# Three one-pass products of split operands for the mixer projections and the embedding gate

## What is computed

```python
h = h + 0.5 * swiglu(rmsnorm(h, ffn1_norm), w_gate, w_up, w_down)    # stage ffn1
u = rmsnorm(h, mix_norm) @ w_in                                      # stage mix1, inputs
c_q, c_kv, k_rope, m_x, m_v, m_o, m_if, f_in = split_cols(u)         # 384,256,64,256,256,256,16,256
y = concat([mla(c_q, c_kv, k_rope), mlstm(m_x, m_v, m_o, m_if), fnet(f_in)])
h = h + y @ w_out                                                    # stage mix1, outputs
h = h + 0.5 * swiglu(rmsnorm(h, ffn2_norm), ...)                     # stage ffn2
e = rmsnorm(p @ ple_w_proj, ple_post_norm)                           # stage ple
h = h + sigmoid(rmsnorm(h, ple_gate_norm) @ ple_w_gate) * e
```

## Time and profile before

| | us |
|---|---|
| median of the runs | 3188.19 |
| the profiled execution | 3193.88 |
| its span, first to last instruction | 3192.1 |
| TensorE busy | 3150.0 (99%) |
| VectorE busy | 1949.2 (61%) |
| ScalarE busy | 1276.8 (40%) |
| float32 products of `xn` and `ring`, 128x256, records | 768 |

### The profile page before, as it was taken

The page is one execution under the profiler, slowest core; times in us unless marked ns, Lnnn a source line. Parts: engine busy times, 40 slices in busy tenths (PEclk is TensorE's granted clock), DMA queues, the critical chain, the costliest instruction groups (busy, mean ns, idle before and its releaser), DMA issues.

```text
span 3192.1 us, 53025 instructions
## 1 busy us (share of the span) xinstructions
PE 3150.0 (99%) x21274; PEld 2685.9 (84%) x21274; DVE 1949.2 (61%) x2974; ACT 1276.8 (40%) x1999; POOL 97.3 (3%) x106
## 2 busy tenths in 40 slices
PE   9999999999999999999999999999999999999999
PEld 8997889889778988888788888878887888876899
DVE  6755574774457556767776677557744676346444
ACT  5444454553345462222544344442224222244433
POOL 0000000000010010000000000000000000000000
PEclk9999999999999999999999999999999999999999
DMA  7543454454345435545222000035532444221353
GB/s 270 184 146 142 175 185 171 178 186 157 139 172 179 176 119 190 185 171 191 93 80 80 3 3 3 28 127 190 205 124 79 171 186 183 97 74 40 134 183 131
DMA packets 62489, 441.25 MB, mean 138 GB/s; under 512 B 6769, under 2 KB 8945, under 8 KB 9329
## 3 DMA queue, kind: packets, MB, share of 16 engines
q1 hardware_dynamic: 60992, 437.39, 37.6%
q10 hardware_dynamic: 1328, 1.46, 0.1%
HBM read 437.77 MB, written 1.05 MB: 137 GB/s over the span
## 4 chain that ended last, share of the span: by engine, by line
PE 91%; DVE 4%; ACT 3%; issue 1%; DMA 0%; POOL 0%; DVEq 0%; ACTq 0%; SPq 0%; POOLq 0%
PE ps_high L526 47%; PE ps_low L526 43%; PE ps_high L535 1%; ACT sb_w_split L774 1%; DVE sb_w_split L811 0%; DVE sb_arena L2151 0%; PE ps_low L535 0%; DVE sb_x_split L2908 0%; ACT sb_arena L2816 0%; DVE sb_silu L2926 0%; ACT sb_xn L2807 0%; DMA sb_ring<-weights 0%; DVE sb_arena L2114 0%; DVE sb_rinv L4495 0%; ACT sb_arena L1972 0%
## 5 line engine op out<-in xcount | busy, mean ns | idle before, releaser
L774 ACT ACTIVATE sb_w_split<-sb_ring 128x2048 fp32r<-128x2048 f32 x260 | 498.6, 1918 | 890.6 <-PE ps_low L526 697.5
L811 DVE TENSOR_TENSOR sb_w_split<-sb_ring,sb_w_split 128x2048 fp32r<-128x2048 f32 x260 | 597.6, 2298 | 257.1 <-ACT sb_w_split L774 257.1
L526 PE MATMUL ps_low<-sb_x_split,sb_w_split 128*128 128x512 f32 (+1 forms) x3520 | 691.2, 354 | 8.3 <-DVE sb_w_split L811 4.0
L526 PE MATMUL ps_high<-sb_x_split,sb_w_split 128*128 128x512 f32 (+1 forms) x3520 | 686.9, 353 | 0.3 <-DVE sb_w_split L811 0.3
L526 PEld LDWEIGHTS ps_low<-sb_x_split,sb_w_split 128*128 128x128 f32 x3520 | 579.0, 189 | 108.0 <-DVE sb_x_split L2908 6.0
L526 PEld LDWEIGHTS ps_high<-sb_x_split,sb_w_split 128*128 128x128 f32 x3520 | 580.3, 189 | 94.7 <-DVE sb_w_split L811 0.6
L526 PE MATMUL ps_low<-sb_a_split,sb_w_split 128*128 128x256 f32 (+1 forms) x2112 | 370.2, 325 | 0.0
L526 PE MATMUL ps_high<-sb_a_split,sb_w_split 128*128 128x256 f32 (+1 forms) x2112 | 365.7, 323 | 0.0
L526 PEld LDWEIGHTS ps_low<-sb_a_split,sb_w_split 128*128 128x128 f32 x2112 | 314.2, 190 | 37.6 <-DVE sb_w_split L811 2.6
L526 PEld LDWEIGHTS ps_high<-sb_a_split,sb_w_split 128*128 128x128 f32 x2112 | 314.9, 190 | 30.9
L1024 DVE SCALAR_TENSOR_TENSOR sb_rest<-sb_ring,sb_consts 128x1024 f32<-128x1024 f32 x256 | 313.3, 1224 | 27.1 <-DVE sb_rest L1024 7.7
(11 more groups left out here) (404 smaller groups left out, 3221.0 us busy)
## 6 DMA issues: line engine op xcount, KB each, us to landing
sb_ring<-weights SPq DMA_DIRECT2D x412, 1024.0 KB, 4.8
sb_consts<-consts SPq DMA_DIRECT2D x1, 2148.0 KB, 18.3
sb_sq<-xT SPq DMA_DIRECT2D x1, 1024.0 KB, 5.6
sb_ring<-weights SPq DMA_DIRECT2D x2, 512.0 KB, 7.5
sb_h<-ctxT ACTq DMA_DIRECT2D x1, 1024.0 KB, 15.5
out<-sb_h SPq DMA_DIRECT2D x1, 512.0 KB, 3.0
sb_vectors<-vectors ACTq DMA_DIRECT2D x1, 269.0 KB, 5.8
out<-sb_h SPq DMA_DIRECT2D x1, 256.0 KB, 2.6
```

The costliest lines, as they stand in the source:

```text
L526: ins = self.g.nc.tensor.matmul(out, lhsT, rhs, start=start, stop=stop)
L774: g.nc.scalar.activation(g.w_split[:, 0, s % 2, :], g.ring[:, n % SLOTS, :], ACT.Copy).then_inc(g.sem["w_high"], 1)
L811: g.nc.vector.tensor_tensor(g.w_split[:, 1, s % 2, :], g.ring[:, n % SLOTS, :], g.w_split[:, 0, s % 2, :].bitcast(F32), ALU.subtract).then ...
```

## The change

In mix1 and ple of the first block, the dense chunks are multiplied with `mm3`. ScalarE splits off the high part into whatever space is free (`w_split`, `a_split`, or a region of the arena, `gates_high`); VectorE writes the low part back over the chunk in its ring slot (`ring_low` is the ring's memory as fp32r). TensorE still releases the slot. The arena's buffers are put in another order so that the new region is free. The new splits are put into the lists by hand. The chunk with the gate columns stays float32; its x is used as two float32 products, high and low.

```diff
+def mixer_split_scalar(act, l, m, first, splits):
+    n = first + MIXER_CHUNKS[m]
+    act.wait_ge(g.landed[n % SLOTS], 16 * (n // SLOTS + 1))
+    if m == 0: act.wait_ge(g.sem["split_used"], splits - 1)
+    elif m == 1: act.wait_ge(g.used[(first - 1) % SLOTS], (first - 1) // SLOTS + 1)
+    elif m == 2: act.wait_ge(g.sem["split_used"], splits)
+    else: act.wait_ge(g.sem["mixer_used"], MIXER_SPLITS * l + m - 1)
+    g.nc.scalar.activation(mixer_high(g, splits, m), g.ring[:, n % SLOTS, :], ACT.Copy)...
+def mixer_split_vector(dve, m, first, splits):
+    dve.wait_ge(g.sem["mixer_high"], dve.due("mixer_high"))
+    g.nc.vector.tensor_tensor(g.ring_low[:, n % SLOTS, :], g.ring[:, n % SLOTS, :],
+                              mixer_high(g, splits, m).bitcast(F32), ALU.subtract)...
+def mixed_high(act, k, source):     # ScalarE: high part of mixed tile k; mixed_low the same on VectorE
...
 # plain_ffn_scalar, behind setup_scalar and after_down
     if kind == "ffn1":
-        plain_prepare_scalar(act, g.vec(f"mix_norm{l}"), ready, split=False)
+        for m in (1, 0):
+            mixer_split_scalar(act, l, m, act.chunks + FFN_CHUNKS, act.splits + FFN_CHUNKS)
+        plain_prepare_scalar(act, g.vec(f"mix_norm{l}"), ready, split=True)
     else:
+        ple_split_scalar(act, 0, act.chunks + FFN_CHUNKS, act.splits + FFN_CHUNKS)
...
 # plain_ffn_vector, behind setup_vector
+    if kind == "ffn1":
+        for m in (1, 0):
+            mixer_split_vector(dve, m, dve.chunks + FFN_CHUNKS, dve.splits + FFN_CHUNKS)
+    else:
+        ple_split_vector(dve, 0, dve.chunks + FFN_CHUNKS, dve.splits + FFN_CHUNKS)
     for j in range(KT):
         residual_add(dve, j, ...)
+        if j:
+            plain_low_parts(dve, g.vec(f"{name}{l}"), j - 1, target, l)
+    plain_low_parts(dve, g.vec(f"{name}{l}"), KT - 1, target, l)
...
 # mix1_tensor: gate columns (x split in two float32 products), every dense chunk, and the outputs
-            pe.mm(tile[...], xn[:, k, t * P:(t + 1) * P], w[:, k * 16:k * 16 + GATE_SPREAD], ...)
+            for n, x in enumerate(mixer_x(g, k, slice(t * P, (t + 1) * P))):
+                pe.mm(tile[...], x.bitcast(F32), w[:, k * 16:k * 16 + GATE_SPREAD], ...)
-            pe.mm(tile[:, 0:TOK], w[:, k, m * P:(m + 1) * P], xn[:, k, 0:TOK], ...)
+            mm3(pe, tile[:, 0:TOK], [part[:, k, m * P:(m + 1) * P] for part in w], mixer_x(g, k), ...)
...
-    pe.wait_ge(g.sem["mix_done"], pe.due("mix_done", 2))
+    pe.wait_ge(g.sem["mixed_low"], pe.due("mixed_low", 4))
     pe.wait_ge(g.sem["low_free"], pe.tiles["low"])
-    out_projection(pe, TOK)
+    mixer_out_projection(pe)
...
 # mix1_scalar: m = 2 behind plain_root, 3 behind the convolution's Silu, 4 behind m_v, 5 and 6
 # behind the latents' squares; then
     root(LH)
+    for k in (6, 7):
+        mixed_high(act, k, g.sq[:, k, 0:TOK])
+    for p in range(2):
+        act.wait_ge(g.sem["mix_done"], act.due("mix_done"))
+        mixed_high(act, 4 + p, g.sq[:, 4 + p, 0:TOK])
+        mixer_split_scalar(act, l, len(MIXER_INPUTS) + p, act.chunks, act.splits)
     ada_units_scalar(act, 0, rows, 1)
...
 # mix1_vector: m = 2, 3 behind the convolution, 4 behind gate_abs, 5 behind gate_exp, 6 behind k_rope; then
     head_out(1)
+    for k in (6, 7, 4):
+        mixed_low_of(k)
+    mixer_split_vector(dve, len(MIXER_INPUTS), dve.chunks, dve.splits)
+    mixed_low_of(5)
+    mixer_split_vector(dve, len(MIXER_INPUTS) + 1, dve.chunks, dve.splits)
     transposed_probs(1)
+    ada_units_vector(dve, 1)
     transposed_probs(2)
+    head_low(0)
+    ada_sum_vector(dve)
     transposed_probs(3)
+    for h in range(1, H):
+        head_low(h)
 # the last two output chunks are split in the eviction loop, on both engines at j = 1 and j = 3
...
 # ple: ScalarE splits 1 inside the embedding's squares, 2 behind plain_root, 3 behind root;
 # VectorE:
+    ple_split_vector(dve, 1, dve.chunks, dve.splits)
     plain_rinv_vector(dve)
     scaled(0)
     scaled(1)
+    ple_split_vector(dve, 2, dve.chunks, dve.splits)
     ...reciprocal(b["rinv_e"], ...)
+    ple_split_vector(dve, 3, dve.chunks, dve.splits)
     finish(0)
```

More of the change, by code:

```diff
@@ L1176, with plain_prepare_scalar @@
 NARROW = slice(TOK, 2 * TOK)
-def plain_prepare_scalar(act, gain, ready, split, between=None):
+def plain_prepare_scalar(act, gain, ready, split, between=None, kind=None):
     g = act.g
@@ new lines, in mixer_split_vector, with mixer_weights @@
+def mixer_split_vector(dve, m, first, splits):
+    g = dve.g
+    n = first + MIXER_CHUNKS[m]
+    dve.wait_ge(g.sem["mixer_high"], dve.due("mixer_high"))
+    g.nc.vector.tensor_tensor(g.ring_low[:, n % SLOTS, :], g.ring[:, n % SLOTS, :],
+                              mixer_high(g, splits, m).bitcast(F32),
+                              ALU.subtract).then_inc(g.sem["mixer_low"], dve.adds("mixer_low"))
+def mixer_weights(pe, m):
+    g = pe.g
+    pe.wait_ge(g.sem["mixer_low"], pe.due("mixer_low"))
+    low = g.ring_low[:, pe.chunks % SLOTS, :]
+    pe.chunks += 1
+    return [part.rearrange("p (k n) -> p k n", k=KT) for part in (mixer_high(g, pe.splits, m), low)]
@@ new lines, in mixer_out_projection @@
+def mixer_out_projection(pe):
+    g = pe.g
+    for c in range(KT // 2):
+        w = mixer_weights(pe, len(MIXER_INPUTS) + c)
+        for m in range(2):
+            pe.wait_ge(g.sem["high_free"], pe.tiles["high"] - 3)
+            tile = pe.open("high")
+            for k in range(KT):
+                mm3(pe, tile[:, 0:TOK], [part[:, k, m * P:(m + 1) * P] for part in w], mixed_parts(g, k), k == 0, k == KT - 1,
+                    full="high" if k == KT - 1 else None)
+        mixer_release(pe)
@@ L1794, in mix1_tensor @@
     feature_tile(w, 1)
-    pe.release()
+    mixer_release(pe)
     decay_rows(2)
@@ L2342, in ple_tensor @@
     plain_sum_tensor(pe)
-    rms_tensor(pe, KT, TOK)
-    for _ in range(KT // 2 - 1):
-        pe.wait_ge(g.landed[pe.chunks % SLOTS], 16 * (pe.chunks // SLOTS + 1))
-        w = pe.chunk(KT, 256)
+    if pe.tiles["low"] >= 4:
+        pe.wait_ge(g.sem["low_free"], pe.tiles["low"] - 3)
+    tile = pe.open("low")
+    for k in range(KT):
+        pe.wait_ge(g.sem["squares"], pe.due("squares"))
+        pe.mm(tile[:, 0:TOK], g.const("ones"), ple_squares(g)[:, k, :], k == 0, k == KT - 1,
+              full="low" if k == KT - 1 else None)
+    for c in range(1, KT // 2):
+        w = ple_weights(pe, c)
         for m in range(2):
@@ L2350, in ple_tensor @@
             for k in range(KT):
-                pe.mm(tile[:, 0:TOK], w[:, k, m * P:(m + 1) * P], g.xn[:, k, 0:TOK], k == 0, k == KT - 1,
-                      full="low" if k == KT - 1 else None)
+                mm3(pe, tile[:, 0:TOK], [part[:, k, m * P:(m + 1) * P] for part in w], ple_x(g, k), k == 0, k == KT - 1,
+                    full="low" if k == KT - 1 else None)
         pe.release()
@@ L2363, in first_projection @@
     for k in range(KT):
-        pe.wait_ge(g.sem["normed"], pe.due("normed"))
+        pe.wait_ge(g.sem["x_split"], pe.due("x_split"))
         for m in range(2):
-            pe.mm(tiles[m][:, 0:TOK], w[:, k, m * P:(m + 1) * P], g.xn[:, k, 0:TOK], k == 0, k == KT - 1,
-                  full="low" if k == KT - 1 else None)
+            mm3(pe, tiles[m][:, 0:TOK], [part[:, k, m * P:(m + 1) * P] for part in w], ple_x(g, k), k == 0, k == KT - 1,
+                full="low" if k == KT - 1 else None)
     pe.release()
```

195 lines of the change are left out of this document (150 added, 45 removed).

## The result

The changed kernel takes 3214.7 us (median of 4 runs, 3212.6 to 3215.8), the kernel before in the same comparison 3190.0 (3186.1 to 3196.6): ratio 1.0078, interval 1.0064 to 1.0093. The forecast was 3206 with a range of 3194 to 3218. Profiled execution against profiled execution the span grew from 3192.1 to 3212.3 us, +20.2, where the prediction's sum gave +17.8. All of it comes ahead of the second block: TensorE's first products there start at 1191.19 instead of 1170.71, +20.5. The medians are further apart, by 24.7; the part on the prediction says why.

What follows compares the result with a forecast made beforehand. TensorE was taken as the bound (busy 99%, 91% of the chain), with VectorE and ScalarE delaying it at certain places; terms summed to +17.8, about +18, on the median 3188: 3206 us, range 3194 to 3218.

Steps and rivals of the forecast that it cites:

- 20 chunks of products: Exposed input and output chunks of mix1: each 0.96 us cheaper (bounds 0.8 and 1.15), -19.2 us.
- gate columns: Gate columns in mix1: 32 records of about 3.5 us double in each layer, +7.0 us.
- entry, layer 0: Entry of mix1: two new splits stand ahead of VectorE's adds; net +5.8, plus 1.9 for the clock, +7.7 us.
- entry, layer 1: Entry of mix1 without set-up: first k starts 1.7 us late, GpSimd's sum of squares sets the norm's product; +1.1 us.
- inside the inputs: Input chunks of mix1: splits ahead of the latents delay rotary and first head products; +1.4 a layer, +2.8 us.
- end of mix1, twice: Low parts and two splits ahead of head 1's copy: +5.9, plus 1.3 for what follows; +7.2 a layer, +14.4 us.
- ple: Splits delay the VectorE and ScalarE chain, the products' 3.8 us gain nothing: 1.2 + 1.9 clock + 0.9, +4.0 us.
- Hidden by 0.5: Mixer outputs: splits of output chunks 2 and 3 ready 0.5 us before they are needed, so no cost.
- rival 4: VectorE becomes the bound inside the inputs too, and the clock falls at each wait: +28, 3216 us; 15%.
- All hidden: Rival 1: everything added is hidden and the kernel is faster, -22, 3166 us; 7%.
- The faster product: Rival 2: products run at the float32 pass rate, 0.108 us, 5.2 us a chunk: +3, 3191 us; 6%.
- The clock that doesn't fall: Rival 3: the clock does not fall, or the stalls overlap with it: +13 to +14, 3201 us; 15%.

Runs made afterwards that it cites:

- outs_early: Changed kernel with the splits of the mixer's first two output chunks moved earlier, heads' copies and mixed low parts behind the transposed probabilities: 3201.2 us, ratio 1.0036.
- outs_evict: outs_early plus high parts of the last two output chunks ahead of the eviction loop, low parts behind the first and third add: 3199.5 us, ratio 1.0036.
- fillers: Changed kernel with extra unread TensorE products in three idle stretches: first pair of layer 0, ffn1 of layer 1, GpSimd's wait: 3211.2 us, ratio 1.0074.
- gates_one_product: Changed kernel with gate columns as one float32 product with the input's high part, not two; output not the reference's: 3209.2 us, ratio 1.0066.
- ple_undone: Changed kernel with the embedding stages (ple) as in the kernel before, mixers keeping the change: 3209.5 us, ratio 1.0060.
- all_moves_fill: all_moves plus unread TensorE products: 5 ahead of the second head's condition sum, 8 instead of 6 ahead of GpSimd's wait: 3179.2 us, ratio 0.9965.
- before_fill: Kernel before, without the change, with the same unread products as all_moves_fill: 3186.7 us, ratio 0.9987.
- all_moves: Changed kernel with the moves of outs_evict, ple_undone and entry_spread together: 3185.5 us, ratio 0.9984.
- entry_spread: Changed kernel with the set-up in pieces behind the down chunks and VectorE's second mixer split behind the input's last low part: 3211.3 us, ratio 1.0071.

## Why the prediction came out as it did

Its mechanism was right and its sum within 2.7 us, but that closeness is partly luck: one term saved 6 us more than forecast, and four small ones were missing or too small.

The medians are 24.7 us apart (3214.7 and 3190.0), not 20.2, and the kernel took 8.7 us more than the 3206 forecast. Of these, 2.6 are the sum: laid on the profiled execution whose rows were read it gives 3211.7, and 3214.3 was measured. The rest is the step from there to the median. The kernel before takes 3186 to 3199 us, with a mean clock from 0.999 down to 0.996, and its profiled execution (3193.88, 0.997) was 5.7 above the median on which the forecast was laid; the changed kernel's (3214.29) lies at its median. So the trace of the kernel before already held losses to the clock that most of its executions don't have, and the changed kernel has them each time (0.990 or 0.991 in all four).

| term | forecast | measured | from |
|---|---|---|---|
| 20 chunks of products | -19.2 | -25.2 | 20 x 1.26, from one chunk of 5.66 us (217.53 to 223.18 in the chain) |
| gate columns | +7.0 | +7.1 | 7.26 for 64 records against 3.68 for 32 |
| entry, layer 0 | +7.7 | +7.0 | +6.7 idle, +0.3 behind it |
| entry, layer 1 | +1.1 | +2.3 | 13.6 - 11.6, and 0.3 in the pair |
| inside the inputs | +2.8 | +4.8 | the rest of the offsets |
| end of mix1, twice | +14.4 | +13.9 | 4.6 to 11.4, 13.1 to 20.2 |
| outputs into ffn2 | 0 | +4.0 | 4 x 1.26 less gives 5.0, seen 4.3; +1.3 wait |
| ple | +4.0 | +6.6 | 8.4 to 11.6, 17.1 to 20.5 |
| sum | +17.8 | +20.5 | |

- **The product** was mis-sized. Chunk after chunk in the down phase a chunk takes 5.96; in the mixer it takes 5.66, 0.118 a record. I had given 1.15 as the most that it could save; it saves 1.26.
- **Entry, layer 0**: the order of events was as forecast to 0.1 us (adds behind two splits, first k at 209.91 against 209.9). The 1.9 for the clock was wrong: it was 0.50 from 208 to 212, but there the pair goes at VectorE's pace of 0.87 us for each k, and half the clock costs 0.3.
- **End of mix1**: right in cause and size, +6.8 and +7.1 against 7.2. The idle of "about 8 us" came in two pieces, 4.48 for ScalarE's `xn`, which stood behind its two splits, and 3.34 for VectorE's copy. outs_early gives 5.8 us of it back in layer 0 by order alone (337.65 to 331.89).
- **"Hidden by 0.5"** is the step that failed. The splits of output chunks 2 and 3 are in time for the products, but I didn't follow them to the next consumer: VectorE waits 2.3 us for ScalarE's high part (L1703 at 346.69 and 352.74), its later adds and low parts are pushed back, and ffn2 waits 1.3. outs_evict takes this away.
- **ple, layer 1**: only a chain of 0.9 was charged and no clock. Measured: 1.4 for the chain, and 1.95 from the product that waits for GpSimd to the second block, at a granted clock of 0.50 (the window's row: length, busy of PE, PEld, DVE, ACT, POOL, clock, DMA):

```profile
1176.00:1188.00 12.00, 9.88 (x32) 8.62 (x33) 4.42 (x9) 7.29 (x18) 1.66 (x2) 0.50 0.27 88
```

- **Inside the inputs**: layer 0 lost 1.6 (1.1 of it at the latent sum), layer 1 3.2. In layer 1 the clock is down for a while between 836 and 844 (mean 0.80), where the kernel before has 1.00; by estimate (8 us at 0.80) 1.6 us of the 3.2 are that, and in fillers, where it did not fall, 1.4 are back. In gates_one_product TensorE is still the bound, so rival 4 is out.
- **Rivals.** All hidden: false as the change stands; with the moves it comes out faster, by a quarter to a third of the 22 us that this rival had (6.2 in the traces, 7.5 in the medians, both kernels with fillers). The faster product: in part true (0.118, between 0.124 and 0.108). The clock that doesn't fall: it fell, after idles of 7.3 and 7.6 us and at the end of mix1, and fillers bring 1.5 and 5 us back.

The Trainium skill's "Back-to-back issue gap" in "TensorE: Matmul & The Clock Gate" would have had 109 ns a product; this trace has 118, so with weight loads the formula is 9 ns low here; my row from the down phase, 124, was 6 ns high.

## What to carry to other kernels

A split of an operand trades TensorE's time for time of two in-order queues, so ask of each of its instructions which instruction stands behind it and who waits for that one, down to the next stage's first product: in the traces the mixers' change with its 11 splits per layer makes the kernel 15 us slower (ple_undone against the kernel before) or 6 us faster (all_moves_fill against before_fill) by their place. Move them to where the engine's own timeline is idle, never as one block longer than the slack of one step. In a stage that ends in a VectorE and ScalarE chain, cheaper products buy idle time and a lower clock.

## What the runs showed of the hardware

- The same products cost 5.96 us a chunk of 48 in the down phase, where they write to eight accumulators in turn, and 5.66 in the mixer, where 24 in a row go to one. The cause wasn't tested.
- An idle of 2.68 us at the end of mix1 left the clock at 1.00 in layer 1 of outs_evict and was followed by 0.50 in layer 0 of the same execution; in layer 1 of all_moves the same idle was followed by 0.50 for 6 us. outs_evict, layers 0 and 1 (the windows' rows):

```profile
326.00:328.00 2.00, 2.00 (x7) 1.54 (x7) 1.64 (x5) 1.72 (x3) 0.00 (x0) 0.50 0.48 201
...
896.00:898.00 2.00, 1.39 (x8) 1.24 (x9) 2.00 (x5) 2.00 (x4) 0.00 (x0) 1.00 0.94 385
```

- The clock can also fall with no long wait: at 255 to 263 in entry_spread, behind a 1.1 us wait and small products, it is 0.79 in the mean. What decides is open; a rule by idle time alone doesn't fit.
- Two more products in an idle of 1.2 us kept the clock at 1.00 and shortened what follows from 11.1 to 8.0 us (1150.81 to 1158.82), since the stretch behind it holds fillers of its own that took twice as long at half clock.
